# Part of a modulation matrix product moved from TensorE fill work in a recurrence to VectorE row sums in three feed-forwards

## What is computed

```python
s_lat = jax.nn.silu(c)[:, None, :]
s_ctx = jax.nn.silu(c_ctx)
for l in range(DEPTH):                       # DEPTH = 2
    ml = jnp.split(s_lat @ w_mod[l] + b_mod[l], N_MOD, axis=-1)   # N_MOD = 9 vectors of 1024
    mc = jnp.split(s_ctx @ w_mod[l] + b_mod[l], N_MOD, axis=-1)
    x = half_ffn(x, g_norm[l, 0], ml[0], ml[1], ml[2], ...)
    ctx = half_ffn(ctx, g_norm[l, 0], mc[0], mc[1], mc[2], ...)
    ...                                      # mixing uses parts 3 to 5, the second half feed-forward 6 to 8
# half_ffn: h + 0.5 * gate * swiglu(rms_norm(h, g) * (1 + scale) + shift)
```

## Time and profile before

| | |
|---|---|
| device time, three runs | 3132.43, 3137.97, 3141.25 us; median 3137.97 |
| the profiled execution | 3134.65 us; its span is 3133.4 us, with 1.25 us around it |
| recurrence scan, four passes | from about 197 to about 414 us of the span |
| half00, half01, half10 | from about 1158, 1880 and 2294 us |
| PE busy over the span | 3004.9 us (96%) |
| DVE busy over the span | 1374.3 us (44%) |
| ACT busy over the span | 582.4 us (19%) |
| chain that ended last | 90% on PE, 5% on DVE, 3% on ACT |
| loads of w_mod | 36 of 2 MB, 8.5 us from issue to landing (median) |

### The profile page before, as it was taken

One profiled execution on the slowest core, in us unless ns is written; L12 is line 12 of the kernel. 1 busy time (PEld: TensorE's weight loads), 2 busy tenths in 40 slices (PEclk: granted clock), 3 DMA queues, 4 the chain that ended last, 5 costly groups with the idle time before them and its releaser, 6 DMA issues.

```text
span 3133.4 us, 43817 instructions
## 1 busy us (share of the span) xinstructions
PE 3004.9 (96%) x18486; PEld 2429.1 (78%) x18486; DVE 1374.3 (44%) x2855; ACT 582.4 (19%) x1339; POOL 37.3 (1%) x60
## 2 busy tenths in 40 slices
PE   8988999999899999999999899999999999999999
PEld 7656778898488978888854447888878888765999
DVE  3264533433523544445222625445244453225675
ACT  1232222113412021100021621010010100124110
POOL 0000000002000000000000000000000000000000
PEclk9999999999999999999999999999999999999999
DMA  6667854366244452222212102222422222331453
GB/s 235 219 227 258 288 173 154 107 190 175 81 131 134 129 175 70 92 64 74 91 56 77 54 28 81 81 75 62 118 83 81 82 73 74 108 90 43 149 150 107
DMA packets 355846, 371.06 MB, mean 118 GB/s; under 512 B 7395, under 2 KB 282228, under 8 KB 355524
## 3 DMA queue, kind: packets, MB, share of 16 engines
q1 hardware_dynamic: 351828, 361.18, 36.5%
q0 software_dynamic: 2208, 5.31, 0.9%
q10 hardware_dynamic: 1616, 1.77, 0.2%
HBM read 367.19 MB, written 1.05 MB: 118 GB/s over the span
## 4 chain that ended last, share of the span: by engine, by line
PE 90%; DVE 5%; ACT 3%; issue 2%; DMA 0%; DVEq 0%; ACTq 0%
PE acc L132 74%; PE aux L132 15%; ACT sb_xn L275 1%; PE aux L2191 1%; DVE sb_work L1924 0%; DVE sb_work L1921 0%; ACT sb_work L1723 0%; ACT sb_work L1725 0%; DVE sb_xn L253 0%; ACT sb_rstd L266 0%; DVE sb_work L1935 0%; ACT sb_rstd L268 0%; DVE sb_work L1703 0%; DMA sb_x<-xT 0%; DVE sb_work L2341 0%
## 5 line engine op out<-in xcount | busy, mean ns | idle before, releaser
L132 PE MATMUL acc<-sb_xn,weights 128*128 128x256 f32 (+2 forms) x5184 | 1211.4, 388 | 16.2 <-DVE sb_xn L253 10.3
L132 PEld LDWEIGHTS acc<-sb_xn,weights 128*128 128x128 f32 x5184 | 942.2, 190 | 239.6 <-issue 118.8
L132 PE MATMUL acc<-sb_work 128*128 128x256 f32 (+1 forms) x1944 | 374.6, 346 | 0.0
L132 PEld LDWEIGHTS acc<-sb_work 128*128 128x128 f32 x1944 | 323.8, 191 | 34.7 <-issue 0.4
L132 PE MATMUL acc<-sb_work,weights 128*128 128x256 f32 (+2 forms) x1508 | 322.4, 361 | 3.2 <-DVE sb_work L1238 1.4
L132 PE MATMUL acc<-sb_big,weights 128*128 128x256 f32 (+1 forms) x1776 | 315.2, 334 | 4.1 <-issue 3.9
L132 PEld LDWEIGHTS acc<-sb_big,weights 128*128 128x128 f32 x1776 | 279.3, 192 | 30.8 <-issue 5.3
L132 PEld LDWEIGHTS acc<-sb_work,weights 128*128 128x128 f32 x1508 | 254.2, 191 | 54.3 <-issue 26.1
L1453 DVE TENSOR_TENSOR sb_work<-weights 128x512 f32<-128x512 f32 (+1 forms) x112 | 99.7, 890 | 160.6 <-PE acc L132 160.6
L1425 ACT COPY sb_work<-acc 128x256 f32<-128x256 f32 (+1 forms) x112 | 38.0, 339 | 704.7 <-PE acc L132 704.7
L132 PE MATMUL aux<-sb_xn,sb_work 128*128 128x256 f32 (+1 forms) x704 | 151.3, 359 | 8.9 <-ACT sb_xn L275 8.9
(11 more groups left out here) (305 smaller groups left out, 2591.8 us busy)
## 6 DMA issues: line engine op xcount, KB each, us to landing
weights<-ffn_w_up SPq DMA_DIRECT2D x88, 1024.0 KB, 7.9
weights<-w_mod SPq DMA_DIRECT2D x36, 2048.0 KB, 8.5
weights<-ffn_w_down SPq DMA_DIRECT2D x48, 1408.0 KB, 7.1
weights<-ffn_w_gate SPq DMA_DIRECT2D x44, 1024.0 KB, 5.4
weights<-w_in SPq DMA_DIRECT2D x8, 2048.0 KB, 8.0
weights<-mix_w_in SPq DMA_DIRECT2D x6, 2048.0 KB, 12.3
weights<-na_w_qkv SPq DMA_DIRECT2D x6, 2048.0 KB, 10.1
weights<-ple_w_gate SPq DMA_DIRECT2D x4, 2048.0 KB, 8.3
```

What stands on the lines that cost most here:

```text
L132: return te.matmul(o, lhsT, rhs, start=start, stop=stop, skip_group_check=True)
```

## The change

The list of blocks becomes 18 of layer 0 and the last three of layer 1: 21 blocks, so 43 steps in place of 73. The first 16 are taken where they were; fill_at then takes 7 steps in each pass in place of 14. The first 60 column tiles (128 outputs each) of layer 1 are computed elsewhere. The host lays that part of the matrix out transposed (w_mod_rows, one output on each row of 1024) and the two conditions as a row repeated on all 128 partitions (cond_rows, 1 MB). Each of half00, half01 and half10 does 20 tiles. Ahead of its normalisation ACT issues three DMAs (the conditions and two tiles of 512 KB), and from iteration 2 to 19 one tile each behind L1425, after a wait for the DVE row that frees the buffer. ACT takes the silu of the conditions (128x2048) in iteration 0. DVE does two rows for a tile (scalar_tensor_tensor of 128x1024 with the sum along the row going to sb_mod), one for each condition: the first ahead of L1524 of iteration i, the second behind L1536 of it. In iteration 20 both rows and one addition of the bias (128x40) stand ahead of the first two 128x1408 weight sums and of L1524.

```diff
--- before.py
+++ after.py
@@ -37,6 +37,8 @@
 IN2 = GQ + 2 * GKV + 3 * CONV + QL + KVL + ROPE
 DECAY_C = math.exp(-0.5)
 RING, SLOT = 4, 4096
+BY_ROWS, ROWS_EACH = 60, 20
 NAT_LOG = "natural_log_exp_and_others"
 
 
@@ -812,9 +814,11 @@
 
 
 
-    mod_blocks = [(q // 2, 2 * turn + q % 2, block(1, banks=(2, 3))) for turn in range(9) for q in range(4)]
+    mod_blocks = [(l, b, block(1, banks=(2, 3))) for l, b in [(0, b) for b in range(18)] + [(1, b) for b in range(BY_ROWS // 4, 18)]]
+    n_mod = len(mod_blocks)
     mod_row, mod_cols = signal("modulation_row_copied"), signal("modulation_columns")
-    mod_row_at, mod_cols_at = mod_row.reserve(36), mod_cols.reserve(36)
+    mod_row_at, mod_cols_at = mod_row.reserve(n_mod), mod_cols.reserve(n_mod)
     mod_rows = (rs_buf, rope[:, 3, :])
 
     def sync_modulation():
@@ -849,7 +853,7 @@
                 ins_ = mm(acc[g.bank][32 * t:32 * t + 32, 0:256], sil[:, k, :], w[:, k, 256 * (t // 2):256 * (t // 2) + 256], False, q >= 4)
             acc_full.on(ins_)
             yield
-        columns(35)
+        columns(n_mod - 1)
         yield
 
     def scalar_modulation():
@@ -870,12 +874,12 @@
                 mod[:, at:at + 4, :].rearrange("p (n c) s -> p c n s", n=2), acc[g.bank][:, 0:8].rearrange("p (c n s) -> p c n s", c=2, n=2),
                 cols("b_mod", 4, at).rearrange("p (n c) -> p c n", n=2).unsqueeze(3).to_broadcast([128, 2, 2, 2]), ALU.add))
 
-        for j in range(36):
+        for j in range(n_mod):
             yield
             if j:
                 add(j - 1)
             yield
-        add(35)
+        add(n_mod - 1)
         yield
 
     class Fill:
@@ -891,10 +895,10 @@
 
 
 
-    MOD_STEPS, MOD_EARLY = 36 * 2 + 1, 16
+    MOD_STEPS, MOD_EARLY = n_mod * 2 + 1, 16
 
     def fill_at(p, point):
-        return min(MOD_STEPS, MOD_EARLY + 14 * p + point * 14 // 18)
+        return min(MOD_STEPS, MOD_EARLY + 7 * p + point * 7 // 18)
 
     def tensor_scan(p, other, ahead):
 
@@ -1293,12 +1297,59 @@
     hook_sq = area(xn, FH * L, 2, T2)
     bank_a, bank_b, bank_c, bank_d, bank_e = acc[0], acc[1], acc[2], acc[3], aux[0]
 
+    row_cond, row_tile = area(work, 8192, 2, D), [area(work, 10240 + D * n, D) for n in range(2)]
+    row_junk = area(big, 20 * T2, D)
+    cond_in, cond_set = signal("row_condition_arrived", 16), signal("row_condition_set")
+    rows_in, rows_done = [signal(f"mod_rows_arrived{n}", 16) for n in range(2)], signal("mod_rows_done")
+    class ModRows:
+        def __init__(self, first):
+            self.first, n = first, ROWS_EACH
+            self.cond, self.silu = cond_in.reserve(1)(0), cond_set.reserve(1)(0)
+            at = [rows_in[i].reserve(n // 2) for i in range(2)]
+            self.arrived = lambda t: (rows_in[t % 2], at[t % 2](t // 2))
+            self.done = rows_done.reserve(2 * n)
+    def scalar_rows_load(R, t):
+        if t >= 2:
+            ac.wait_ge(rows_done.sem, R.done(2 * (t - 2) + 1))
+        n0 = 128 * (R.first + t)
+        rows_in[t % 2].on(ac.dma_start(row_tile[t % 2], ins["w_mod_rows"][n0:n0 + 128, :]))
+    def scalar_rows_begin(R):
+        cond_in.on(ac.dma_start(row_cond.rearrange("p s k -> p (s k)"), ins["cond_rows"]))
+        for t in range(2):
+            scalar_rows_load(R, t)
+    def scalar_rows_cond(R):
+        ac.wait_ge(cond_in.sem, R.cond)
+        cond_set.on(ac.activation(row_cond, row_cond, ACT.Silu))
+    def vector_row(R, t, s):
+        if s == 0:
+            if t == 0:
+                ve.wait_ge(cond_set.sem, R.silu)
+            sig, value = R.arrived(t)
+            ve.wait_ge(sig.sem, value)
+        else:
+            ve.wait_ge(rows_done.sem, R.done(2 * t))
+        rows_done.on(ve.scalar_tensor_tensor(row_tile[t % 2] if s else row_junk, row_tile[t % 2], 1.0, row_cond[:, s, :],
+                                             ALU.mult, ALU.mult, accum_out=mod[:, 72 + R.first + t, s:s + 1]))
+    def vector_rows_bias(R):
+        ve.wait_ge(rows_done.sem, R.done(2 * ROWS_EACH - 1))
+        m = mod[:, 72 + R.first:72 + R.first + ROWS_EACH, :]
+        v_step.on(ve.tensor_tensor(m, m, cols("b_mod", ROWS_EACH, 72 + R.first).unsqueeze(2).to_broadcast([128, ROWS_EACH, 2]), ALU.add))
     class Fast:
 
 
 
-        def __init__(self, t0, up=True, hid_at=None):
-            self.t0 = t0
+        def __init__(self, t0, up=True, hid_at=None, rows=None):
+            self.t0, self.rows = t0, rows
             W = self.W = T2 - t0
             H = self.H = W // 2
             n = self.n = FT + KT // 2
@@ -1423,11 +1474,15 @@
             elif j >= 2:
                 ac.wait_ge(st_x.sem, F.x(4 * (i - 2 - FT) + 3))
             st_u.on(ac.copy(u[:, s, :], bank_a[:, 0:F.H]))
+            if F.rows and 2 <= i < ROWS_EACH:
+                scalar_rows_load(F.rows, i)
             if i < FT:
                 ac.wait_ge(st_c12.sem, F.c12(j))
                 st_g2.on(ac.activation(g2[:, s, :], g2[:, s, :], ACT.Silu))
                 ac.wait_ge(F.done[i, 2][0].sem, F.done[i, 2][1])
                 st_g1.on(ac.activation(g1[:, s, :], bank_a[:, 0:F.H], ACT.Silu))
+                if F.rows and i == 0:
+                    scalar_rows_cond(F.rows)
             elif i > FT and following is not None:
                 scalar_square(following, 2 * (i - FT) - 2)
                 scalar_square(following, 2 * (i - FT) - 1)
@@ -1507,6 +1562,11 @@
                 vector_weight_sums(F, i + 1, (3,))
             elif i == 0:
                 vector_weight_sums(F, i + 1, (0, 1, 2, 3))
+            if F.rows and 1 <= i <= ROWS_EACH:
+                vector_row(F.rows, i - 1, 0)
+                if i == ROWS_EACH:
+                    vector_row(F.rows, i - 1, 1)
+                    vector_rows_bias(F.rows)
             if i == FT - 2:
                 vector_weight_sums(F, FT, (0, 1))
             if down >= 0:
@@ -1534,6 +1594,8 @@
                 ve.wait_ge(st_c21.sem, F.c21(j))
                 ve.wait_ge(st_g1.sem, F.g1(i))
                 st_hid.on(ve.tensor_tensor(F.hv[:, i, 0:F.H], g1, u, ALU.mult))
+                if F.rows and 1 <= i < ROWS_EACH:
+                    vector_row(F.rows, i - 1, 1)
 
 
     hid_l, hid_w = area(big, 0, FT, L), area(big, 0, FT, T2)
@@ -1940,12 +2002,12 @@
     half_gate = small[:, 48:64].rearrange("p (k s) -> p k s", s=2)
 
     class HalfFfn:
-        def __init__(self, l, j, t0, x_ready, extra=None, squares=None, hooked=False):
+        def __init__(self, l, j, t0, x_ready, extra=None, squares=None, hooked=False, rows=None):
             self.l, self.j = l, j
             m0 = self.m0 = 72 * l + (0 if j == 0 else 48)
             self.norm = Norm(t0, xv_l if t0 else xv_w, lambda k, h: gsc[:, k, h:h + 1], x_ready, lambda k, h: mod[:, m0 + k, h:h + 1],
                              extra, squares, hooked)
-            self.fast = Fast(t0)
+            self.fast = Fast(t0, rows=rows)
             self.x_ready = self.fast.x_ready
 
     def vector_scales(l, n, m0):
@@ -1965,6 +2027,8 @@
         tensor_fast(F.fast, F.norm.ready, following)
 
     def scalar_half_ffn(F, following=None):
+        if F.fast.rows:
+            scalar_rows_begin(F.fast.rows)
         scalar_norm(F.norm)
         scalar_fast(F.fast, following)
 
@@ -2347,10 +2411,10 @@
     near = Neighbours(ple0.x_ready)
     ffn1 = ConvFfn(1, near.x_ready)
     ple1 = Ple(1, ffn1.x_ready)
-    half00 = HalfFfn(0, 0, 0, ple1.x_ready, extra=(ctx_in, 32))
+    half00 = HalfFfn(0, 0, 0, ple1.x_ready, extra=(ctx_in, 32), rows=ModRows(0))
     mix0 = Mixing(0, True, half00.x_ready, hooked=True)
-    half01 = HalfFfn(0, 1, 0, mix0.x_ready, squares=area(big, 0, KT, T2))
-    half10 = HalfFfn(1, 0, 0, half01.x_ready, squares=hook_sq, hooked=True)
+    half01 = HalfFfn(0, 1, 0, mix0.x_ready, squares=area(big, 0, KT, T2), rows=ModRows(ROWS_EACH))
+    half10 = HalfFfn(1, 0, 0, half01.x_ready, squares=hook_sq, hooked=True, rows=ModRows(2 * ROWS_EACH))
     mix1 = Mixing(1, False, half10.x_ready, hooked=True)
     half11 = HalfFfn(1, 1, CTX, mix1.x_ready, squares=area(big, 0, KT, L))
 
@@ -2612,6 +2676,9 @@
     flat = lambda t: t.reshape(DEPTH, t.shape[1], -1)
     arrays["w_uq"] = np.concatenate([flat(uq[..., 0:NOPE]), flat(uq[:, :, (0, 2, 1, 3, 4, 4, 5, 5), NOPE:])], axis=-1)
     arrays["w_ukv"] = np.concatenate([flat(ukv[..., 0:NOPE]), flat(ukv[..., NOPE:])], axis=-1)
+    arrays["w_mod_rows"] = a["w_mod_2"][1].T[0:128 * BY_ROWS]
+    arrays["cond_rows"] = np.broadcast_to(np.concatenate([a["c_ctx_2"].reshape(-1), a["c_2"].reshape(-1)]), (128, 2 * D))
     arrays.update(tables())
     return {k: np.ascontiguousarray(v) for k, v in arrays.items()}
```

## The result

The changed kernel takes 3094.82 us (median of 4 runs, 3092.97 to 3097.77), the kernel before 3138.78 beside it (4 runs, 3132.43 to 3141.25). The ratio is 0.9864, with a 95% interval of 0.9847 to 0.9881: **faster by 44 us**, where 28 were forecast. A second set of runs gave 0.9883 (0.9863 to 0.9903), 37 us; its median, 3099.73, lies inside the range. Between the two profiled executions it is 36.9 us of span (3133.4 to 3096.5), against 25.7 in the sum; the profiled execution of after (3097.77) is the slowest of its four and that of before (3134.65) faster than three of its four, which is why the profiles show less than the medians.

The account below looks back on a forecast made before the run. PE was taken to bound the kernel, 90% of the chain that ended last. Passes -30.9, clock +2, rows +0.2, issues +3.0 gave -25.7 us: 3109.0 from 3134.65, put at 3110, range 3096 to 3129.

Parts of the forecast that it names:

- where it comes from, level by level: Four recurrence passes: fewer PE fill steps give back 7.7, 6.7, 7.1 and 9.4 us, 30.9 of 38 removed.
- points 2 and 4: Fill places ahead of level 1 in a pass: an A and a B step go, winning 2.4 us in pass 0.
- worth nothing in themselves: Recurrence: no fill step waits for a DMA, so removing 15 w_mod loads of 2 MB gains 0.
- The first rival: Passes: everything comes back, PE-bound throughout or unexplained gaps shrinking with less traffic and fewer instructions; 3096 us, 8%.
- the clock: Passes: less fill brings two more stretches of PE at 1.2 GHz, costing 2 us, between 0 and 10.
- the sign that was set for being wrong: Four passes: the forecast is wrong if the granted clock row falls under 0.9; 0.93 or more was expected.
- The clock rival: Passes: granted clock falls to one half for half of PE's own work, costing 60 us; 3168 us, 5%.
- the rows: Half feed-forwards: 120 DVE rows of 1.45 us hide in idle gaps; 0.2 us lost in all, at iteration 20.
- The half-rate rival: Half feed-forwards: DVE rows run at half throughput, about 2.35 us each, adding 4.8 us and 0.4; 3114 us, 6%.
- the issues at the starts: ACT's three DMA issues ahead of normalisation: 1.5 us in half00, hidden in half01, 1.5 in half10; 3.0 together.
- only points 2 and 12 pay: Passes are bound by DVE and ACT more than read, gaining 15 us less 5; 3125 us, 13%.
- steps pile up behind the passes: Recurrence: the change doesn't bite, fill steps leaving the passes but piling up behind them; 1%.

Follow-up runs that it names:

- e3: The kernel before with 15 of the 36 w_mod loads cut to an eighth, all PE work kept: 3126.75 us, ratio 0.9975.
- e4: The changed kernel with 15 more 2 MB transfers on SP's queue from w_mod to memory nobody reads: 3102.02 us, ratio 0.9897 against the kernel before.
- e5: The changed kernel with ACT's first DMA issues of each stage moved later, behind squares and table load (half10: before the last square): 3088.46 us, again 3090.87.
- After again: The changed kernel itself, unaltered, in a second set of runs beside the kernel before: 3099.73 us, ratio 0.9883.
- e9: e5 with only the eight blocks ahead of the recurrence, thirteen left out as zeros, no fill in the passes: 3086.44 us, ratio 0.9851 against before.
- e8: e5 with all 72 tiles of layer 1 by rows, 24 a stage, and 21 fill steps in the passes for 27: 3094.83 us, ratio 0.9870 against before.
- e2: The kernel before with its whole fill kept and the rows added in the feed-forwards: 3139.05 us, ratio 1.0006.
- e6: The kernel before with seven fill steps in each pass and the other 29 behind the last pass: 3168.45 us, ratio 1.0100.

## Why the prediction was right, and by how much not

**Right: where it comes from, level by level.** The start of the five level products P, measured from the start of pass 0 (199.72 before, 194.77 after), was 4.65, 10.61, 17.30, 22.41 and 30.57 us and is 2.35, 8.33, 13.91, 19.02 and 25.42. They are earlier by 2.3, 2.3, 3.4, 3.4 and 5.2 us. The steps gave 2.4 (points 2 and 4), 0, 1.1, 0 and 1.8, so 2.4, 2.4, 3.5, 3.5 and 5.3. The level starts in after show what was said to come late next:

```profile
203.10 1.15 PE L134 MATMUL aux<-sb_big,sb_xn 64*64 64x64 f32 x32 [0.49 <-DVE sb_big L1105]
...
208.68 1.15 PE L134 MATMUL aux<-sb_big,sb_xn 64*64 64x64 f32 x32 [0.36 <-DVE sb_big L1105]
...
213.79 1.15 PE L134 MATMUL aux<-sb_big,sb_xn 64*64 64x64 f32 x32 [1.19 <-DVE sb_big L1105]
```

**The step that failed** is the sentence that the loads which go away "are worth nothing in themselves", and with it the sum, which left the gaps without a cause as they were. It looked only for waits that name a DMA. e3, with the loads alone cut, is 8.4 us faster, and the gaps of its pass 1 are gone. But pass 0 is another matter. Behind level 5, pass 0 should have given another 2.4 us and gave 6.2: the gap of 1.97 us ahead of 241.68 and the slow fill step behind it, 0.9 longer than others, are not there any more. Those make 2.9 of the 3.8 too much, and they went with the steps: e3, without the loads, has that gap still, and e4, with them, has not. Taken over the passes, gaps without a cause fell by 6.3 us in this pair of profiles, and by 4 to 6 over all of them. Pass 2, which had no such gap (clock 1.00), gave 7.3 against 7.1 forecast; pass 1 gave 8.9 against 6.7, pass 0 11.4 against 7.7, pass 3, where a gap of 2.6 stood, 11.1 against 9.4; from another pair of profiles single passes come out by up to 3 us otherwise, so only the sum carries weight. That the loads drive a part of this is shown by e3's time (8.4 us, between 4 and 12); in its one profile the passes are 3.7 shorter, of the 9.8 by which after's beat the forecast. The first rival named exactly this ("the unexplained gaps shrink with less traffic and fewer instructions") at 8%; it should have been a term of the forecast.

**Mis-sized: the clock.** I took 2 us off for new slow stretches. The granted clock is 1.00, 0.97, 1.00 and 0.97, no lower than before. One slow step stands in pass 1, behind a gap of 1.92 us, as in before behind one of 2.09. That is this profile, though. e5's, with the same steps, has pass 1 at a clock of 0.87 and 52.60 us long: behind a gap of 2.74 us its 64 matmuls at the end take 3.69 us. After again has a gap of 2.73 at the same place, takes 1.98 for them, and its pass 1 is 48.35 us at 1.00. So the sign that was set for being wrong, a clock under 0.9, did show in one pass of one profile of six, and cost about 4 us there: within the 0 to 10 that were allowed. The clock rival (3168) didn't come. What speaks for it came over several passes only when more was taken away: e9's first two passes ran at 0.82 and 0.85 with the same DVE work, and even so the whole was not slower. The Trainium skill's warning (TensorE: Matmul & The Clock Gate, HAM oscillation — how this bites in real kernels) describes e8 and e9, where the slow stretches follow waits of 2.0 to 2.2 us in pass 0 and the waits of 1.2 us in the same pass have none, better than this change.

**Right: the rows.** 1.30 us each where 1.45 was taken; hidden; period unchanged; nothing in iteration 20. There L1584 starts at 1390.48 and ends at 1390.90, and product 7 starts at 1392.07 without a wait, 1.2 us behind it where 0.6 was worked out, since the rows and the bias (2 x 1.3 + 0.2) were shorter than the 3.2 taken. The half-rate rival is out: 1.22 us for 1024 elements is what a plain tensor_tensor takes, although both sources are f32 in SBUF and the sum is taken along. On this the measurement decides against the Trainium skill's Vector Engine (DVE) Microarchitecture Reference, Points that are easy to get wrong.

**Nearly right: the issues at the starts.** Forecast 1.5 for half00, none for half01, 1.5 for half10. Measured in the profile: half00 3.0, of it 1.5 (2.45 - 0.99) in the wait and 1.5 (8.83 - 7.28) in the squares at the lower clock, which I had not counted; half10 1.0, the gap ahead of the table load, which answers to the earlier trace rows:

```profile
2260.89 1.25 ACTq L1320 DMA_DIRECT2D sb_work<-w_mod_rows  x2
2262.18 1.28 ACT L266 ACT_TABLE_LOAD   x1 [1.03 <-issue]
```

Together 4.0 for 3.0. e5's profile has all 4.0 back (wait 1.06, squares 7.20, no gap ahead of the table load); its times are 5 to 9 less, and the rest stays open.

**The account of the two profiles**, in us of span: ahead of pass 0 -5.0 (chance, see e2); passes -38.7; half00's start +3.0, half10's +1.0; iteration 20 0; matmuls behind the same waits at the starts of half01 and half11 +1.7 and +1.6, where only the granted clock differs. That is chance: after again has at both starts matmuls as fast as before's (1.96 and 1.13 us for the first eight, where after takes 2.45 and 1.84). The sum is -36.4, of 36.9 measured. Against the forecast's -25.7, the passes differ by -9.8 (-38.7 less -28.9), the stretch ahead of them by -5.0, the starts by +1.0 and the chance of the clock by +3.3.

**The other rivals.** That only points 2 and 12 pay (3125) is out, by the level starts. That steps pile up behind the passes is out too; e6 shows what it would have cost, 32 us and not the few that the PE work alone suggests.

**Open.** What PE lacks in the gaps without a cause, and how the 9.8 divide: the gap and slow step of pass 0 (2.9) go with the steps, the gaps of pass 1 with the loads, and no run has fewer instructions alone in the other passes. How much adding the loads again (e4) costs, 4 to 10 us with wide intervals. How much of e8's loss is the two tiles in one iteration: no run has these alone.
